# Expert gate products as float32r with 256 columns per token, and the work around them moved between VectorE, ScalarE and GpSimd

## The reference, cut to what matters

```python
    eidx = jnp.take_along_axis(cidx, pos, axis=-1)      # i1 * 128 + i2
    g = jax.nn.softmax(top_s, axis=-1)
    u_sel = jnp.take(u, eidx, axis=0)
    a = jax.nn.gelu(jnp.einsum('chkd,cd->chk', u_sel, xc), approximate=False)
    w = (g * a).astype(x.dtype)
    v_sel = jnp.take(v, eidx, axis=0)
    return jnp.einsum('chk,chkd->cd', w, v_sel)
```

## Time and profile before

| | us |
|---|---|
| median of 3 runs | 2511.76 (2506.16 to 2512.29) |
| profiled execution: span | 2506.7 |
| gate stage of each layer, first gate matmul to the last | 205 |
| TensorE busy | 2415.1 (96%) |
| VectorE busy | 1745.4 (70%) |
| ScalarE busy | 1343.7 (54%) |
| GpSimd busy | 710.7 (28%) |

### The profile page before, as it was taken

The page is one execution under the profiler, slowest core; times in us unless marked ns, Lnnn a source line. Parts: engine busy times, 40 slices in busy tenths (PEclk is TensorE's granted clock), DMA queues, the critical chain, the costliest instruction groups (busy, mean ns, idle before and its releaser), DMA issues. The chain is left out here.

```text
span 2506.7 us, 57329 instructions
## 1 busy us (share of the span) xinstructions
PE 2415.1 (96%) x16509; PEld 2210.5 (88%) x16509; DVE 1745.4 (70%) x3945; ACT 1343.7 (54%) x2396; POOL 710.7 (28%) x564
## 2 busy tenths in 40 slices
PE   7999999999999999999999999999999999899998
PEld 6889999999888888888999999988888887688996
DVE  5647777887777777564777788777777767556346
ACT  3545555676555555454455567665555543434443
POOL 5665444000000000566544400000000043134665
PEclk9999999999999999999999999999999999999999
DMA  6244566444566666623466644556666644432454
GB/s 242 89 145 167 211 230 225 164 155 171 186 236 245 238 243 237 244 85 138 166 217 223 229 164 152 182 175 247 234 247 236 243 161 155 144 135 105 176 189 151
DMA packets 98053, 475.31 MB, mean 190 GB/s; under 512 B 11808, under 2 KB 13344, under 8 KB 50720
## 3 DMA queue, kind: packets, MB, share of 16 engines
q1 hardware_dynamic: 97392, 472.91, 52.9%
q10 hardware_dynamic: 560, 1.19, 0.1%
HBM read 438.41 MB, written 35.65 MB: 189 GB/s over the span
## 5 line engine op out<-in xcount | busy, mean ns | idle before, releaser
L1414 ACT ACTIVATE wh<-ring 128x512 fp32r<-128x512 f32 x1428 | 882.1, 627 | 621.4 <-ACTq L1413 617.9
L2102 DVE TENSOR_TENSOR wl<-ring,wh 128x512 fp32r<-128x512 f32 x961 | 672.7, 705 | 275.0 <-DVEq L2101 257.2
L1099 PE MATMUL PS<-xh,wh 128*128 128x256 f32 x2048 | 593.9, 290 | 6.9 <-PEq L1095 5.4
L1099 PE MATMUL PS<-xl,wh 128*128 128x256 f32 x2048 | 579.9, 283 | 0.0
L1099 PE MATMUL PS<-xh,wl 128*128 128x256 f32 x2048 | 579.9, 283 | 0.0
L510 POOL TENSOR_TENSOR wl<-ring,wh 128x512 fp32r<-128x512 f32 x295 | 391.2, 1349 | 292.9 <-POOLq L509 289.4
L895 PE MATMUL PS<-wh,xh 128*128 128x512 f32 x1088 | 425.3, 391 | 2.2 <-PEq L892 2.2
L895 PE MATMUL PS<-wh,xl 128*128 128x512 f32 x1088 | 423.5, 389 | 0.0
L895 PE MATMUL PS<-wl,xh 128*128 128x512 f32 x1088 | 423.4, 389 | 0.0
L1099 PEld LDWEIGHTS PS<-xh,wh 128*128 128x128 f32 x2048 | 392.7, 192 | 12.8 <-issue 12.1
L1099 PEld LDWEIGHTS PS<-xl,wh 128*128 128x128 f32 x2048 | 393.3, 192 | 0.0
(11 more groups left out here) (339 smaller groups left out, 3817.4 us busy)
## 6 DMA issues: line engine op xcount, KB each, us to landing
ring<-in_peer_u SPq DMA_DIRECT2D x128, 1024.0 KB, 4.8
ring<-in_peer_v SPq DMA_DIRECT2D x128, 1024.0 KB, 4.8
acts<-stg SPq DMA_DIRECT2D x124, 256.0 KB, 2.1
gains<-acts SPq DMA_DIRECT2D x124, 256.0 KB, 4.9
ring<-in_w_in SPq DMA_DIRECT2D x24, 1024.0 KB, 4.9
ring<-in_w_gate_up SPq DMA_DIRECT2D x22, 1024.0 KB, 4.8
ring<-in_peer_wq SPq DMA_DIRECT2D x16, 1024.0 KB, 4.8
ring<-in_w_down SPq DMA_DIRECT2D x11, 1024.0 KB, 4.8
```

What stands on the lines that cost most here:

```text
L1099: last = pe.matmul(PS[:, 2 * j, 0:S], w[:, q, k * P:(k + 1) * P], x[:, at, :], start=at + i == 0, stop=at + i == 9)
L1414: act.activation(wh[:, q, :], ring[:, s, q * QW:(q + 1) * QW], ACT.Copy).then_inc(high_ready[q], 1)
L2102: part = dve.tensor_tensor(wl[:, q, :], ring[:, s, q * QW:(q + 1) * QW], wh[:, q, :].bitcast(F32), SUB)
```

## The change

In the gate stage of both layers:

- The gate is split into a high and a low part (`gparts`, float32r). Now one matrix `rowhot[pick, i1]` holds 0 or 1, and `colhot[pick, 2, i2]` holds the gate's two parts. TensorE makes one float32r product of 256 columns per token, into two banks per group.
- VectorE builds `colhot` with four `scalar_tensor_tensor` of 256 elements per group. It builds `rowhot` with one comparison for groups in slot 0. For slot 1 ScalarE builds it (`rowhots`): four `Abs` of 128 elements, a drain and a `Relu` of 512.
- ScalarE copies only the low halves out (`gate_lows`, to a packed buffer). VectorE adds high and low into the arena (`gates_in`).
- GpSimd makes all four low parts of the last 25 chunks; VectorE makes none.
- The chunks carry 3, 2, 3, 2, ... groups, the last two carry 2.
- Small tiles move into the free quarter of `sel` and `selT`, with no other instructions.

```diff
@@ GpSimd
                 pool.sem_inc(pool_lows_done, 1)
+                pool.wait_ge(picks_ready, 1)
+                pool.sem_inc(picks_ready, -1)
+                low_rest(NPAIR - N_GATE, 4)
+                pool.sem_inc(pool_lows_done, 1)
                 pool.wait_ge(dve_lows_done, 1)
@@ TensorE, gates(s)
                     pe.wait_ge(oneh_ready, 1)
                     pe.sem_inc(oneh_ready, -1)
+                    if s:
+                        pe.wait_ge(rowhot_ready, 1)
+                        pe.sem_inc(rowhot_ready, -1)
                     pe.wait_ge(slot_free[2 + s], 1)
                     pe.sem_inc(slot_free[2 + s], -1)
                     for n in range(4):
-                        last = pe.matmul(PS[:, 4 + 2 * s, n * P:(n + 1) * P], ohA[:, s, n, :], ohB[:, s, n, :],
-                                         start=True, stop=True)
+                        last = pe.matmul(ps2(2 + s)[:, 2 * n * P:2 * (n + 1) * P], rowhot[:, s, n, :],
+                                         colhot[:, s, n, :, :].rearrange("p i k -> p (i k)"), start=True, stop=True)
                     last.then_inc(act_full[2 + s], 1)
@@
                 with pe.Fori(0, 6):
                     experts((0, 1, 0))
+                    experts((1, 0))
                     experts((1, 0, 1))
-                with pe.Fori(0, 14):
+                    experts((0, 1))
+                with pe.Fori(0, 2):
                     experts((0, 1))
@@ ScalarE
-                def gates_out(at, s):
+                def gate_lows(s, at=None):
 
                     act.wait_ge(act_full[2 + s], 1)
                     act.sem_inc(act_full[2 + s], -1)
-                    act.sem_inc(oneh_used[s], 1)
-                    act.activation(av[:, bass.ds(at, 4), :], PS[:, 4 + 2 * s, :].rearrange("p (n e) -> p n e", n=4),
-                                   ACT.Copy).then_inc(slot_free[2 + s], 1)
+                    act.activation(gains0[:, s, 0:4 * P].rearrange("p (n e) -> p n e", n=4),
+                                   ps2(2 + s).rearrange("p (n i e) -> p n i e", n=4, i=2)[:, :, 1, :],
+                                   ACT.Copy).then_inc(lows_out[s], 1)
+                    if s and at is not None:
+                        rowhots(at + 8)
+
+                def rowhots(at):
+
+                    for n in range(4):
+                        act.activation(rowhot[:, 1, n, :], iota[:, :], ACT.Abs, scale=-1.0,
+                                       bias=selT[:, 0, bass.ds(at + n, 1)])
+                    act.drain()
+                    act.activation(rowhot[:, 1, :, :], rowhot[:, 1, :, :].bitcast(F32), ACT.Relu, scale=-1.0,
+                                   bias=ones[:, 0:1]).then_inc(rowhot_ready, 1)
@@ VectorE
-                    dve.tensor_copy(selT[:, :, t * P:(t + 1) * P],
-                                    ps2(2 + t)[:, 0:3 * P].rearrange("p (i n) -> p i n", i=3)
-                                    ).then_inc(slot_free[2 + t], 1)
+                    mine = slice(t * P, (t + 1) * P)
+                    dve.tensor_copy(selT[:, 0:2, mine], ps2(2 + t)[:, 0:2 * P].rearrange("p (i n) -> p i n", i=2))
+                    own(dve.tensor_copy(gparts[:, 0, mine], ps2(2 + t)[:, 2 * P:3 * P]))
+                    own(dve.tensor_tensor(gparts[:, 1, mine], ps2(2 + t)[:, 2 * P:3 * P],
+                                          gparts[:, 0, mine].bitcast(F32), SUB))
+                    dve.sem_inc(slot_free[2 + t], 1)
                 low(0, 3, 2)
-                own(dve.engine_nop())
+                dve.sem_inc(picks_ready, 1)
+                dve.sem_inc(picks_act, 1)
 
                 def onehots(at, s):
 
-                    dve.wait_ge(oneh_used[s], 1)
-                    dve.sem_inc(oneh_used[s], -1)
-                    dve.tensor_tensor(ohB[:, s, :, :], bc(iota[:, :].unsqueeze(1), 4, P),
-                                      bc(selT[:, 1, bass.ds(at, 4)].unsqueeze(2), 4, P), ALU.is_equal)
+                    if s == 0:
+                        own(dve.tensor_tensor(rowhot[:, s, :, :], bc(iota[:, :].unsqueeze(1), 4, P),
+                                              bc(selT[:, 0, bass.ds(at, 4)].unsqueeze(2), 4, P), ALU.is_equal))
+                    else:
+                        own(dve.engine_nop())
                     for n in range(4):
-                        last = dve.tensor_scalar(ohA[:, s, n, :], iota[:, :], selT[:, 0, bass.ds(at + n, 1)],
-                                                 selT[:, 2, bass.ds(at + n, 1)], ALU.is_equal, MUL)
+                        last = dve.scalar_tensor_tensor(colhot[:, s, n, :, :], bc(iota[:, :].unsqueeze(1), 2, P),
+                                                        selT[:, 1, bass.ds(at + n, 1)],
+                                                        bc(gparts[:, :, bass.ds(at + n, 1)].bitcast(F32), 2, P),
+                                                        ALU.is_equal, MUL)
                     last.then_inc(oneh_ready, 1)
 
-                def lows(s, at, slots):
...
+                def gates_in(at, s):
+
+                    dve.wait_ge(lows_out[s], 1)
+                    dve.sem_inc(lows_out[s], -1)
+                    highs = ps2(2 + s).rearrange("p (n i e) -> p n i e", n=4, i=2)[:, :, 0, :]
+                    lows = gains0[:, s, 0:4 * P].rearrange("p (n e) -> p n e", n=4)
+                    dve.tensor_tensor(av[:, bass.ds(at, 4), :], highs, lows, ADD).then_inc(slot_free[2 + s], 1)
+
+                def gates(at, slots):
+
+                    for i, s in enumerate(slots):
+                        gates_in(at + 4 * i, s)
+                        onehots(at + 4 * i + 8, s)
 
                 for s in (0, 1):
                     onehots(4 * s, s)
                 with dve.Fori(0, 6) as i:
-                    for k in range(2):
-                        lows(1 - k, 24 * i + 12 * k + 8, (k, 1 - k, k))
+                    gates(40 * i, (0, 1, 0, 1, 0, 1, 0, 1, 0, 1))
+                gates(S - 16, (0, 1))
                 for s in (0, 1):
-                    dve.wait_ge(oneh_used[s], 1)
-                    dve.sem_inc(oneh_used[s], -1)
-                dve.wait_ge(gates_done, 1)
-                dve.sem_inc(gates_done, -1)
+                    gates_in(S - 8 + 4 * s, s)
+                own(dve.engine_nop())
+                dve.sem_inc(oneh_done, 1)
+                dve.wait_ge(pool_lows_done, 1)
+                dve.sem_inc(pool_lows_done, -1)
```

More of the change, by code:

```diff
@@ L116, in build @@
         oneh = peer_k[:, 4:6, :].rearrange("p a b -> p (a b)").rearrange("p (a b) -> p a b", b=TOPK)
[L117 to L127, removed]
+        rowhot = nc.alloc_sbuf_tensor_at("rowhot", [P, 2, 4, P], F32R, offset=sel_at)
+        colhot = nc.alloc_sbuf_tensor_at("colhot", [P, 2, 4, 2, P], F32R, offset=gains0_at)
+        gparts = nc.alloc_sbuf_tensor_at("gparts", [P, 2, S], F32R, offset=selT_at + 2 * S * 4)
         stg = sb("stg", [P, 2, 2 * S])
@@ L175, in build @@
         evac_done = sem("evac_done")
-        oneh_ready = sem("oneh_ready")
+        oneh_ready, rowhot_ready = sem("oneh_ready"), sem("rowhot_ready")
+        picks_act = sem("picks_act")
         pool_lows_done = sem("pool_lows_done")
@@ L185, in build @@
         cast_ready = [sem(f"cast_ready{j}") for j in (0, 1)]
-        oneh_used = [sem(f"oneh_used{s}") for s in (0, 1)]
-        gates_done = sem("gates_done")
+        lows_out = [sem(f"lows_out{s}") for s in (0, 1)]
+        picks_ready = sem("picks_ready")
         wst_ready = [sem(f"wst_ready{s}") for s in (0, 1)]
@@ L1643, in expert, with experts @@
                         act.sem_inc(acts_kept[s] if kept else acts_out[s], 1)
-                def experts(c, s, first=False, kept=False, at=None, slots=()):
+                def experts(c, s, first=False, kept=False, slots=(), at=None):
                     high(s, 0)
@@ L1650, in experts @@
                     if slots:
-                        gates_out(at, slots[0])
+                        gate_lows(slots[0], at)
                     high(s, 2)
                     if len(slots) > 2:
-                        gates_out(at + 4, slots[1])
+                        gate_lows(slots[1], at + 4)
                     expert(c - 1, 1 - s, 1, kept=kept)
@@ L1679, in _ @@
                 experts(N_ROUTE + 2, 0)
+                act.wait_ge(picks_act, 1)
+                act.sem_inc(picks_act, -1)
+                rowhots(4)
                 with act.Fori(0, 6) as i:
-                    for k in range(2):
[L1682 to L1686, removed]
+                    for k, (at, slots) in enumerate(((0, (0, 1, 0)), (12, (1, 0)), (20, (1, 0, 1)), (32, (0, 1)))):
+                        experts(4 * i + N_GATE + 1 + k, 1 - k % 2, slots=slots, at=40 * i + at)
+                experts(NPAIR - 1, 1, kept=True, slots=(0, 1), at=S - 16)
                 for j in range(2):
                     expert(NPAIR - 1, 1, j, kept=True)
-                    gates_out(S - 8 + 4 * j, j)
-                act.drain().then_inc(gates_done, 1)
```

(14 more changed lines are left out.)

33 lines of the change are left out of this document (19 added, 14 removed).

## The result

The changed kernel took 2654.33 us (median of 4 runs, 2653.16 to 2664.28) beside 2512.03 us (4 runs) for the kernel before: a ratio of 1.0578, 95% interval 1.0557 to 1.0599. It is slower by 5.8%. The forecast was 2711 us in a range of 2590 to 2800, slower with a chance of 0.89: the direction and the range held, and the centre was 57 us too high.

What follows compares the result with a forecast made beforehand. TensorE bounded the kernel before; VectorE was to bound the gate stage after. Per layer 301 + 4 - 205.7 = +99.3 us, two layers +199; 2506.7 + 5.1 + 199 = 2711 us, range 2590 to 2800.

Steps and rivals of the forecast that it cites:

- TensorE's gain: Gate stage: a gate group falls from 0.81 to 0.48 us on TensorE, about 25 us per layer on offer.
- VectorE as the new pace: Gate stage: VectorE's queue sets the pace at 4.7 us per group, 301 us per layer; chance 0.78.
- the collision term: Gate stage: GpSimd's low parts hold up VectorE's colhot and rowhot, 1.4 us per group, bounds 0.9 and 1.8.
- VectorE's own 3.3 us: Gate stage: VectorE's undisturbed time per group, colhot 1.56, rowhot 0.35, own wait 0.33 and gates_in 1.05 us.
- Entry of the stage: Start of the gate stage: longer preparation before the first gate group costs 4 us per layer.
- ScalarE not the bound: Gate stage: ScalarE needs 3.0 us per group, near TensorE's 2.82 and under VectorE's time.
- The loop ... has a whole group time of slack: Gate stage: the loop TensorE, gate_lows, gates_in adds nothing to the time.
- The 3, 2, 3, 2 distribution changes no total: Gate stage: the uneven number of groups per chunk adds no time.
- the faster rival: Gate stage: TensorE stays the bound with VectorE under 2.82 us per group, -21.2 us per layer, 2469 us; chance 0.07.
- mostly hidden: Gate stage: VectorE bounds, but low parts fall mostly where they cost nothing, +19 us in all, 2530 us; chance 0.08.
- the one with the clock: Gate stage: TensorE granted only 1.2 GHz throughout becomes the bound, +159 us per layer, 2831 us; chance 0.05.
- the two with a gain or none: Gate stage: TensorE's gain comes through, 2469 us, chance 0.07; or faster matmuls and slower VectorE cancel, chance 0.02.

Runs made afterwards that it cites:

- e1: The changed kernel with iota copied once per layer to a free PSUM bank, where VectorE's colhot and rowhot read it: 2543.05 us, ratio 1.0123.
- e2: The changed kernel with the low parts of the last 26 chunks back on VectorE and GpSimd idle in the stage: 2666.3 us, ratio 1.0611.
- e4: The changed kernel with VectorE building rowhot for both slots and ScalarE's rowhots gone: 2697.24 us, ratio 1.0733.
- e5: e1 without VectorE's wait for its own last result (separate semaphore for rowhot, colhot tokens 2 and 3 built first): 2534.98 us, ratio 1.0095.
- e12: The changed kernel with only the gate groups reordered to stand 2, 1, 2, 1, 2 quarters apart: 2648.68 us, ratio 1.0564.
- e10: e5 with the gate groups 2, 1, 2, 1, 2 quarters apart instead of 2, 1, 1, 2, 2: 2509.49 us, ratio 0.9999.
- e6: e1 with only two of four colhot instructions per group after the first groups, leaving out half the tokens' gates: 2509.6 us, ratio 0.9992.
- e3: The changed kernel with gates_in writing packed results, leaving out the scattered layout later steps read: 2636.94 us, ratio 1.0497.

## Why the prediction was right, and where its size was off

- **TensorE's gain was real and never arrived.** Four matmuls for 0.47 us against 0.81 before; 0.48 was forecast. But the engine stood still for 137 us in the two stages, about three times the 43 it saved.
- **VectorE as the new pace: right.** Forecast 4.7 us per group, measured 4.31. The step that was mis-sized is the collision term, "Weighted: 0.87 us, x 1.6 = 1.4 us per group". Against e1's undisturbed means, `colhot` lost 4 x (706 - 477) ns = 0.92 us per group, and `rowhot` (1069 ns mean) half of 1069 - 685, 0.19: 1.11 us. With 100 low parts in 64 groups that is 0.71 us per low part. The share was taken rightly: of the 99 low parts that start inside the first layer's stage, 58 start while VectorE is in a one-hot instruction, as the assumed 1.9 of 3.3 says. So was the full price of a hit. The averages over the hits were not. Counted from the starts and lengths in the trace (what each held instruction took above e1's mean), the 38 low parts that start in one of the first three `colhot`s of a group cost 1.04 us each. But the 12 that start in `rowhot`, with VectorE's own wait behind it, cost 0.70, and the 8 that start in the fourth `colhot`, with `gates_in` behind it, 0.12. Together these 58 cost 0.85 us each, not 1.1; the 38 that start in `gates_in` cost 0.48, not 0.55.
- **VectorE's own 3.3 us:** 4.31 - 1.11 = 3.20. e1 gives 3.22 (212.0 us less the 9.3 it waited before `gates_in`), e2 3.14 (263.3 less 65 for the low parts). The terms: `gates_in` 1.06 (forecast 1.05), own wait 17.5 / 63 = 0.28 (0.33), `colhot` 0.47 undisturbed (0.47).
- **The 57 us between 2711 and 2654:** 0.39 us x 63 intervals x 2 layers = 49. Another 9 are a slip in the working: 64 groups were counted, though the first one's VectorE work lies ahead of the first gate group, where the entry had it already. Small terms of both signs are left.
- **Entry of the stage:** forecast 4 us per layer, measured 5.0 and 4.7 (first gate group at 459.84 instead of 454.86).
- **ScalarE not the bound: right,** with 170 of 272 us busy and 43 us more without its help (e4).
- **TensorE's clock:** it stood at 0.94 and 0.95 in these windows, so the stretch of the earlier trace rows that kept 1.00 with 14.93 of 21 us busy was no guide to this stage. TensorE was busy for 204 us, where 180.5 were reckoned. It did not set the stage's length here, since VectorE never waited before `gates_in`. In e2, at 0.89, VectorE did wait there, 13 us per stage, and in e5 the clock counted too.
- **"The loop ... has a whole group time of slack" and "The 3, 2, 3, 2 distribution changes no total":** true for the changed kernel (no wait before `gates_in`; e12 moves it by 6 us, with overlapping intervals), false as a statement about the scheme. As soon as the collisions are out, both show: 25 us between e5 and e10. They would also have made the faster rival fail: it needed VectorE under 2.82 us per group, and e6, with about 2.5, only drew level.
- **Of the rivals,** "mostly hidden" (2530) fell by `colhot`'s rows, the one with the clock (2831) by the windows, the two with a gain or none by the time. The forecast was right by its reason, not by luck: e1 removes that reason alone and 111 of 142 us go with it.

Open are the last stops of e10; a shorter queue for `gate_lows` on ScalarE, or a third slot that would loosen the loop, was not tried.

## What to carry to other kernels

Before work is moved to GpSimd, look at what VectorE does in that stretch: if its instructions have two tensor inputs in SBUF, the move can cost VectorE as much as it saves (here 1.1 us per group against 1.0), and here one constant operand copied to PSUM took that cost away. Price a saving on one engine by the next engine's time per unit of work, and, once that has room too, by the loop through all engines over the closest two units, not by the average distance. A gain in a part that covers another's collisions comes only in part (e3: 17 of 47 us).

## What the hardware showed that I had not expected

- A VectorE instruction with a broadcast input in PSUM, a second input in SBUF and a per-partition operand in SBUF kept its 0.472 to 0.487 us in all 512 cases beside GpSimd's products. The Trainium skill, page "SBUF — State Buffer", section "Who interferes with whom", names two SBUF inputs as the condition; e1 agrees, and adds that the per-partition operand does not count as one. Its "whole instruction" is longer than what the rows show: the instruction at 565.12 ends 0.28 us behind a low part, 0.19 us less than its own 0.47.
- A float32r matmul of 128 columns takes 0.84 / 8 = 0.105 us in a row of eight, one of 256 columns 0.47 / 4 = 0.12: half the columns saved 0.01 us.
- The scattered destination (512 elements, 256 floats apart) costs VectorE 0.38 us (1060 against 680 ns), 0.7 ns per element.
